# Scaling the experts' input once, and moving work between engines in both mixers of a three-layer model

## The reference, cut to what matters

```python
# layer 0: sparse attention and a state-space mixer side by side, then a gated feed-forward
h = rmsnorm(x) @ in_w                        # q, latent, index keys and queries, z, xbc, dt
y_a = attention over the 64 positions that an index score chooses (16 head-and-tile steps)
xbc = silu(causal_conv4(xbc) + conv_b)       # 12 chunks of 128 channels; then the chunked scan
x = x + concat(y_a, y_b) @ out_w
x = x + (silu(h @ w_gate) * (h @ w_up)) @ w_down
# layer 1: gated short convolution of 3 taps, then a feed-forward; final norm
x = x + (gate_b * causal_conv3(gate_c * v)) @ out_w
# layer 2: gated linear recurrence (y_a) and dilated window attention (y_b)
merged = sigmoid(ga) * (y_a @ w_branch_a) + sigmoid(gb) * (y_b @ w_branch_b)
x = x + merged @ w_out
h2 = rms_norm(x, norm2_g)
q = h2 @ peer_wq                             # 8 heads, two halves of 64
top 16 of 128 keys in each half, top 16 of the 256 sums, softmax gates
x = x + sum over experts of gelu(u[e] . h2) * gate * v[e]      # 16384 experts, all computed
```

## Time and profile before

| | us |
|---|---|
| median of 3 runs (1762.32 to 1766.17) | 1765.11 |
| the profiled execution | 1763.7 |
| its span | 1762.0 |
| TensorE busy | 1714.8 |
| ScalarE busy | 973.2 |
| VectorE busy | 1046.8 |
| GpSimd busy | 1060.3 |

### The profile page before, as it was taken

How to read it: one execution, slowest core, us unless ns; L and a number is a source line. 1 busy time by engine, 2 the same in 40 slices (tenths; PEclk the granted TensorE clock), 3 DMA queues, 4 the chain that set the end, 5 groups by cost and what they waited for, 6 DMA issues and landing times.

```text
span 1762.0 us, 32340 instructions
## 1 busy us (share of the span) xinstructions
PE 1714.8 (97%) x10886; PEld 1539.4 (87%) x10886; DVE 1046.8 (59%) x2232; ACT 973.2 (55%) x1840; POOL 1060.3 (60%) x828
## 2 busy tenths in 40 slices
PE   8989999999999999999999999999999999999999
PEld 8778788889978887989989999999999988888887
DVE  3775433336753335563532888836999866666776
ACT  5556655555455556665536545455555555555554
POOL 8435799997979998975527989897666400000000
PEclk9999999999999999999989999999999999999999
DMA  6223455554545554543424545555454555556775
GB/s 233 96 89 106 155 189 189 183 188 161 186 149 187 190 187 159 200 136 120 154 77 165 169 159 186 164 173 168 162 166 156 163 191 190 193 189 215 239 240 169
DMA packets 91852, 299.01 MB, mean 170 GB/s; under 512 B 10208, under 2 KB 22624, under 8 KB 91520
## 3 DMA queue, kind: packets, MB, share of 16 engines
q1 hardware_dynamic: 91152, 293.64, 50.4%
q0 software_dynamic: 480, 4.35, 0.7%
q10 hardware_dynamic: 144, 0.08, 0.0%
HBM read 290.69 MB, written 7.34 MB: 169 GB/s over the span
## 4 chain that ended last, share of the span: by engine, by line
PE 76%; POOL 11%; issue 6%; DVE 4%; ACT 3%; DMA 0%; POOLq 0%; DVEq 0%; SPq 0%; ACTq 0%
PE bank L683 53%; POOL w_lo L627 11%; PE bank L713 9%; PE bank L714 5%; PE bank L1298 3%; PE bank L661 1%; PE bank L1239 1%; ACT w_hi L1344 1%; PE bank L759 1%; PE bank L773 0%; DMA ring<-stream 0%; PE bank L1248 0%; DVE arena L2047 0%; PE bank L899 0%; PE bank L879 0%
## 5 line engine op out<-in xcount | busy, mean ns | idle before, releaser
L627 POOL TENSOR_TENSOR w_lo<-ring,w_hi 128x512 fp32r<-128x512 f32 x804 | 1052.7, 1319 | 334.3 <-ACT w_hi L1344 293.6
L1344 ACT ACTIVATE w_hi<-ring 128x512 fp32r<-128x512 f32 x1060 | 664.9, 632 | 641.5 <-PE bank L683 521.7
L683 PE MATMUL bank<-h_high_and_low,w_hi 128*128 128x256 f32 x3552 | 671.5, 287 | 19.7 <-POOL w_lo L627 11.7
L683 PEld LDWEIGHTS bank<-h_high_and_low,w_hi 128*128 128x128 f32 x3552 | 565.8, 193 | 24.8 <-POOL w_lo L627 12.8
L683 PE MATMUL bank<-h_high_and_low,w_lo 128*128 128x256 f32 x1776 | 505.4, 285 | 0.0
L683 PEld LDWEIGHTS bank<-h_high_and_low,w_lo 128*128 128x128 f32 x1776 | 343.3, 193 | 0.7 <-issue 0.5
L683 PE MATMUL bank<-w_hi,A_hi 128*128 128x512 f32 x728 | 287.6, 395 | 4.1 <-DVE A_lo L2221 2.8
L683 PE MATMUL bank<-w_hi,A_lo 128*128 128x512 f32 x728 | 286.5, 393 | 0.0
L683 PE MATMUL bank<-w_lo,A_hi 128*128 128x512 f32 x728 | 283.7, 390 | 0.0
L713 PE MATMUL bank<-h_high_and_low,w_hi 128*128 128x512 f32 x704 | 250.2, 398 | 0.0
L2557 DVE TENSOR_TENSOR w_lo<-ring,w_hi 128x512 fp32r<-128x512 f32 x256 | 177.1, 693 | 112.8 <-ACT w_hi L1344 111.9
(11 more groups left out here) (362 smaller groups left out, 1672.5 us busy)
## 6 DMA issues: line engine op xcount, KB each, us to landing
ring<-stream SPq DMA_DIRECT2D x530, 512.0 KB, 3.3
spill<-mask_parts SPq DMA_DIRECT2D x48, 128.0 KB, 1.7
XN<-spill SPq DMA_DIRECT2D x48, 128.0 KB, 4.7
arena<-branch_w POOLq DMA_DIRECT2D x1, 3072.0 KB, 10.3
X<-x SPq DMA_DIRECT2D x2, 512.0 KB, 4.5
arena<-kv_w SPq DMA_DIRECT2D x1, 1024.0 KB, 7.4
out<-X SPq DMA_DIRECT2D x4, 256.0 KB, 2.1
arena<-row POOLq DMA_DIRECT2D x1, 512.0 KB, 4.8
```

Of the source, the lines that this page charges most:

```text
L627: nc.gpsimd.tensor_tensor(w_lo[:, hs, :], ring[:, slot(phase, e), k * HALF:(k + 1) * HALF], w_hi[:, hs, :].bitcast(F32), ALU.subtract) \
L683: last = mm(dst, a, b, start=start and n == 0, stop=stop and n == 2, skip_group_check=True)
L1344: A(w_hi[:, half_slot(phase, e, k), :], ring[:, slot(phase, e), k * HALF:(k + 1) * HALF], ACT.Copy).then_inc(rounded, 1)
```

## The change

- First mixer: `conv` is cut in two. `scaled_input` stays on VectorE; the first tap with the bias becomes one ScalarE instruction, `first_tap`; VectorE waits for it and does the `later_taps`. `CONVS` gives the slot of each chunk. Chunks 6 and 7 go to banks 2 and 3, `cb` to bank 1. The choice of positions spreads over slots 0 to 4. On ScalarE, `conv_silu` moves from the head of slots 6 and 9 to their end, and `decay(0)` to the end of slot 10; on TensorE `cb` moves to slot 7, `cumulated(0)` to 9 and the turned inputs to 10.
- Norms: a one-column Sqrt on an unused tile `warm` stands before `high`; for the feed-forwards and the short convolution each of the two squares is followed by half of a `follow`.
- Short convolution: products and gate stay in PSUM, and ScalarE's copy of the gate is gone.
- Second mixer: the recurrence's logarithm and exponentials are halved and put behind single halves of units; outputs, sums and reciprocals come earlier; the load of `branch_w` is issued behind gate unit 12; the branch products go between the last attention steps and between the rows of `l2_out`.
- Experts: the factor is spread after four of the eight query units; `rescaled` multiplies the transposed input in PSUM, ScalarE rounds it, VectorE takes the low part, and `early` waits for it. The scaling of 128 results goes, and Gelu reads PSUM.

```diff
-X_BANKS = (6, 7, 2, 3, 6, 7, 6, 7, 6, 7, 6, 7)
+X_BANKS = (6, 7, 2, 3, 6, 7, 2, 3, 6, 7, 6, 7)
...
-    out += [("acs", 1, 1), ("BT", 1, 1), ("cb", 3, 1), ("ab0", 3, 1), ("xsT0", 1, 1), ("xsT2", 2, 1)]
+    out += [("acs", 1, 1), ("BT", 1, 1), ("cb", 1, 1), ("ab0", 3, 1), ("xsT0", 1, 1), ("xsT2", 2, 1)]
...
+        CONVS = ((), (), (0,), (1,), (2,), (3,), (4,), (5,), (6,), (7, 8), (9,), (10,))
...
+                        if p.name == "l2_gates" and e == 12:
+                            pool.wait_ge(ev("ya_ready"), 1)
+                            pool.dma_start(branch_w, br_w).then_inc(ev("branch_loaded"), 16)
                 else:
...
                         transposes("BT", [CV[:, 8 + g, 0:P] for g in range(2)])
+                    if u == 7:
                         pe.wait_ge(*before_turn("cb"))
...
+                    if u == 9:
                         cumulated(0)
-                    if u == 9:
+                    if u == 10:
                         inputs_turned(0)
...
-                        output_sums(u // 2 - 2)
+                    if u in (0, 1):
+                        outputs(u)
+                    if u in (2, 3):
+                        output_sums(u - 2)
                     if u == 1:
...
+                pe.wait_ge(ev("ya_ready"), 1)
+                pe.wait_ge(ev("branch_loaded"), 16)
+                branch_a(0)
+                attention_step("dil", NT * 4, NT * 4, logits, values)
+                branch_a(1)
+                attention_step("dil", NT * 4 + 1, NT * 4, logits, values)
+                branch_a(2)
+                pe.wait_ge(*read_out("dil_o6"))
+                pe.wait_ge(*read_out("dil_o7"))
+                transposes("ybT", [YB[:, t, cc * P:(cc + 1) * P] for cc in range(2) for t in range(NT)])
+                branch_a(3)
+                pe.wait_ge(*read_out("ybT"))
+                branch_b(0)
+                branch_b(1)
+                for k in range(4):
+                    pe.wait_ge(*before_turn(f"acc5_{k}"))
+                out_rows(0)
+                branch_b(2)
+                out_rows(1)
+                branch_b(3)
                 out_rows(2)
                 out_rows(3)
...
+                    if i == 0:
+                        spread_scale(6)
...
+                for j in range(4):
+                    pe.wait_ge(*read_out(f"hT6_{j}"))
...
+            def norm_late(n, gain, name=None):
+                A(warm[:], epst[:], ACT.Sqrt)
                 high(n, gain)
-                squares()
-            def squares():
                 for t in range(NT):
-                    A(XN[:, t, :], X[:, t, :], ACT.Square, accum_out=stat[:, t:t + 1]).then_inc(ev("ssq"), 1)
+                    square(t)
+                    if name:
+                        follow(f"{name}_head", 0, 0, (t,))
...
+                    cc = (8 + u) % 12
+                    act.wait_ge(ev("x_scaled"), u + 1)
+                    A(CV[:, cc, :], bank(f"xu{u}")[:, 0:S], ACT.Identity, bias=vcol("xbc_b", cc),
+                      scale=vcol("xbc_w", cc * 4 + 3)).then_inc(ev("first_tap"), 1)
...
                     steps = dsa_steps(u)
+                    follow("l0_feature", 4 + u, 0, (0,))
+                    for n in CONVS[u]:
+                        first_tap(n)
+                    if len(steps) == 2:
+                        attend(steps[0])
+                    follow("l0_feature", 4 + u, 0, (1,))
+                    attend(steps[-1])
                     if u == 6:
                         conv_silu(0)
                     if u == 9:
                         conv_silu(1)
                     if u == 10:
                         decay(0)
-                    follow("l0_feature", 4 + u, 0, (0,))
-                    if len(steps) == 2:
-                        attend(steps[0])
-                    follow("l0_feature", 4 + u, 0, (1,))
-                    attend(steps[-1])
                     if u == 4:
                         act.wait_ge(ev("acs_diff"), 1)
                         A(dts[:, 144:160], dts[:, 112:128], ACT.Exp)
...
                 def body(phase, e, q, turn, i, j):
-                    follow(phase, e, i)
                     if phase == f"{name}_head":
                         root(n)
+                    else:
...
-                    act.wait_ge(*unit_used(phase, e + 2, i))
-                    A(SCG[:, q, 1, :], bank(f"sc_gate{q}")[:, 0:S], ACT.Copy).then_inc(*frees(f"sc_gate{q}"))
...
                         A(qn[:], qn[:], ACT.Sqrt, bias=eps64[:]).then_inc(ev("q_rms"), 1)
+                def decay_log(j):
+                    act.wait_ge(ev("hg_f"), 1)
+                    A(HG.rearrange("p (h t) -> p h t", h=4)[:, 2 * j:2 * j + 2, :], F2[:, 2 * j:2 * j + 2, :],
+                      ACT.Ln).then_inc(ev("hg_log"), 1)
...
+                    act.wait_ge(ev("hg_sums"), 1)
+                    if j < 2:
+                        A(HT[:, half], HS[:, half], ACT.Exp).then_inc(ev("hg_exp"), 1)
+                    else:
+                        A(YA[:, half], HS[:, half], ACT.Exp, scale=-1.0).then_inc(ev("hg_exp"), 1)
...
-                    follow("l2_mix", 2 * p)
-                    if p == 6:
-                        recurrent(5)
-                    follow("l2_mix", 2 * p + 1)
+                    for e in (2 * p, 2 * p + 1):
+                        for half in range(2):
+                            follow("l2_mix", e, 0, (half,))
+                            if e == 10:
+                                decay_log(half)
+                            if p == 6:
+                                decay_exp(2 * (e % 2) + half)
                     mix_used(p)
-                    if p != 5:
-                        recurrent(p)
+                    recurrent(p)
...
                     A(F2[:, 24 + 2 * j:26 + 2 * j, :], F2[:, 24 + 2 * j:26 + 2 * j, :], ACT.Sigmoid)
...
+                for p in range(2):
+                    act.wait_ge(*read_out(f"gates{p}", 3))
+                gate_sigmoid(0)
+                attention_step("dil", NT * 4, LG1, PT1, DIL_WIDTHS)
+                gate_sigmoid(1)
+                act.wait_ge(*full("ybT"))
+                A(YBT.rearrange("p c t -> p (c t)"), bank("ybT")[:], ACT.Copy).then_inc(*frees("ybT"))
+                for j in (2, 3):
...
+                    if j < 4:
+                        act.wait_ge(ev("h_scaled"), j + 1)
+                        A(h_hi[:, 2 * j:2 * j + 2, :], bank(f"hT6_{j}")[:].rearrange("p (c t) -> p c t", t=S),
+                          ACT.Copy).then_inc(ev("scaled_high"), 1)
                     act.wait_ge(*full(f"ps{j}"))
...
                     follow(phase, at % 4, at // 4)
-                    if u >= 1:
-                        activated(u - 1)
+                    act.wait_ge(*unit_used(phase, at % 4, at // 4))
+                    A(chunk(GATED + u), bank(f"early{u % 4}")[:, 0:S], ACT.Gelu).then_inc(*frees(f"early{u % 4}"))
...
-                        act.wait_ge(*read_out(f"build{c % 3}", c // 3))
-                        A(stage[:, c % STAGED, :], stage[:, c % STAGED, :], ACT.Gelu).then_inc(ev("staged"), 1)
+                        if c >= STAGED:
+                            act.wait_ge(ev(f"spilled{c % STAGED}"), 16 * (c // STAGED))
+                        act.wait_ge(*unit_used("peer_build", e, i))
+                        A(stage[:, c % STAGED, :], bank(f"build{c % 3}")[:, 0:S],
+                          ACT.Gelu).then_inc(*frees(f"build{c % 3}"))
...
+                if n == 2:
                     chain(V.tensor_copy(RB1, bank(f"rb{n}")[:, 0:S]))
                     chain(V.tensor_tensor(RB, RB1, bank(f"rb{n}")[:, 0:S], ALU.mult))
                 else:
                     chain(V.tensor_copy(RB, bank(f"rb{n}")[:, 0:S]))
...
+            def rescaled(n, gain):
+                dve.wait_ge(ev("query_low"), 4)
+                for j in range(4):
+                    for c in range(2):
+                        v = bank(f"hT{n}_{j}")[:, c * S:(c + 1) * S]
+                        ins = V.scalar_tensor_tensor(v, v, vcol(gain, 2 * j + c), RB, ALU.mult, ALU.mult)
+                    ins.then_inc(ev("h_scaled"), 1)
+                for j in range(4):
+                    pair = slice(2 * j, 2 * j + 2)
+                    dve.wait_ge(ev("scaled_high"), j + 1)
+                    V.tensor_tensor(h_lo[:, pair, :], bank(f"hT{n}_{j}")[:].rearrange("p (c t) -> p c t", t=S),
+                                    h_hi[:, pair, :].bitcast(F32), ALU.subtract).then_inc(*frees(f"hT{n}_{j}"))
             def add_to_residual(n, phase, e, i=0):
                 for h in range(2):
...
+                def scaled_input(u):
+                    v = bank(f"xu{u}")[:, 0:S]
+                    dve.wait_ge(*unit_used("l0_feature", 4 + u))
+                    V.tensor_tensor(v, RB, v, ALU.mult).then_inc(ev("x_scaled"), 1)
+                def later_taps(u):
                     cc, name = (8 + u) % 12, f"xu{u}"
                     v, o = bank(name)[:, 0:S], CV[:, cc, :]
```

(61 more changed lines are left out.)

183 lines of the change are left out of this document (70 added, 113 removed).

## The result

The changed kernel takes 1769.73 us (median of 11 runs, 1768.87 to 1771.23); the kernel before, in the same series, 1764.25. The ratio is 1.0029, with an interval of 1.0021 to 1.0036: slower by 0.3%, where 0.4% faster was forecast. The profiled execution took 1768.9 us, its span is 1767.2, so 5.2 more than before.

A forecast was written before the change was run, and what follows sets the result against it. The prediction took TensorE to bound the kernel, busy 1714.8 of 1762.0 us. Terms 2.0 - 4.6 + 2.3 - 2.5 - 5.5 + 1.6 + 0 = -6.7 gave 1757.0 profiled, 1758.4 as median; range 1742 to 1767.

The forecast's parts named there:

- the one that gave the late stages nothing: `build` and `peer_late`: TensorE busy for 414.3 of 415 us, so sparing VectorE there is worth nothing; no term.
- Every sign that the prediction named for being right: Named waits in slots 6 and 7, loads ahead of `high`, branch products between attention steps, `w_lo` waits remaining, short-convolution wait gone.
- First mixer: Old waits and slow clock give 12.6 us, new waits, mostly for ScalarE, take 14.6: net +2.0, bounds -12.6 and +5.
- The 1.3 us that I took off: First mixer: new waits sum to 15.9 us, taken as 14.6 because a wait lets the others catch up.
- Short convolution: End of the short convolution: the wait of 2.8 us and 1.84 of slow matmuls go, -4.6, bounds -5 to -2.
- Norms: Norms: the table load before `high` falls on TensorE's path at two norms; +2.3 us in all, bounds 0 and +3.5.
- the slack of 0.6: Short convolution's norm: TensorE has about 0.6 us of slack against the 1.28 load, leaving +0.7.
- Second mixer: Recurrence and key sums: shorter waits, -2.5 us; branch products filling attention's waits at the end, -5.5.
- Experts: Hand-off before `early`: +1.6 us, bounds 0 and +4; 80 scaled results of `early` removed: 0, bounds -11.7 and +3.
- The rival that they were ScalarE's: `early`: its stalls are ScalarE's waits and vanish with the slow clock, -11.7 us, 1746.7; chance 0.17.
- the rival of 1767: `early`: GpSimd never gets its turn between two comparisons, 9 us with the clock; counted as no change, chance 0.14.
- the slower rival: First mixer: `first_tap` waits for VectorE's scaled input, each of 12 slots loses 1.2 us, +14, 1772; chance 0.08.

The follow-up runs named there:

- e2: Kernel before the change with an unused one-column tile ahead of `A_hi`, shifting it by 32 bytes: 1773.81 us, ratio 1.0055.
- e1: Changed kernel with `warm` declared behind the arena, so `A_hi` and `A_lo` lie where they lay before: 1759.25 us, ratio 0.9973 to the kernel before.
- e12: e1 with the first tap of the first mixer's convolution back on VectorE: 1755.47 us, ratio 0.9951 to the kernel before.
- e10: e1 with the old first mixer, except chunk 6 in bank 2 (later banks adapted) and the choice over five slots: 1752.73 us, ratio 0.9933.
- e6: e1 without the tile `warm` and the Sqrt on it ahead of `high`: 1758.37 us, ratio 0.9967 to the kernel before.
- e8: e1 with VectorE's 2048-element comparisons and products in the experts' choice cut into four of 512: 1752.95 us, ratio 0.9931.
- e3: Kernel before the change with an unused 16-column tile ahead of `A_hi`, putting it on a multiple of 128 bytes: 1761.94 us, ratio 0.9980.

## Why the prediction was wrong

**The step that failed is the one that gave the late stages nothing.** The prediction took the pace of a unit of rows for fixed, "that is the pace wherever nobody waits", and asked of each edit only which wait it removes or adds. The declaration of `warm` was read as nothing at all. It costs 8.3 us by the stretches: 6.8 in the last 128 units, where nobody waits, and 1.5 in the 52 rows units before. e2 shows it alone (9.6 us by the medians), e1 takes it out (10.5). With it out, the change measures 1759.25, beside a forecast of 1758.4; with it, 1769.73, over the 1767 at which the range ended. That e1 comes so near is in part luck: against their terms the first mixer is 3.9 us and the norms are 1.7 too slow there, `early` is 2.0 and `l2_mix` 1.5 too fast. Every sign that the prediction named for being right came true, and none of its signs looked at the pace of a unit.

**First mixer: the mechanism right in the main, the size wrong**, +6.3 by its stretch where +2.0 was taken. The waits for ScalarE came at the named places: at `BT` 1.5 us, behind 1.6 for VectorE that ended while ScalarE was at its table load (together 3.1, forecast 3.5), `cb` 2.3 (2.4), slot 10 2.5 (3.2); the wait at the z units was 2.8 (1.9). In the prediction's own terms, the waits were to grow by 1.6 us, from 9.4 to 11.0; TensorE's idle time in this stretch grew by 3.9, from 9.5 to 13.5. The 1.7 us of waits for VectorE's masked logits in slots 5 and 6 I had not seen; they stay in e12, so the handing over of first taps isn't their cause, and e10 has such waits too. The clock was to cost 1.7 net, and TensorE's busy time grew by 2.4: the granted clock is at half speed for 10.2 us of the stretch in both kernels, but before TensorE was idle for 3.6 of them (84.4 to 87.9 and 91.3 to 98.1 us) and now for 0.9 (95.7 to 102.5 and 106.0 to 109.4). The 1.3 us that I took off because a wait lets the others catch up are not there. e10 measures what the useful edits are worth in the old order: 3.5 us by the stretch, since waits for VectorE take back part.

**Short convolution: right**, -4.4 by its stretch and -4.7 in e1, for -4.6. From 420 to 506 us TensorE is busy throughout.

**Norms: too small.** The waits for `h_lo` are 1.7 and 1.5 (forecast 0.7 and 1.4), and the squares cut apart add 0.5 at each feed-forward: about 4 for 2.3, beyond its upper bound of 3.5. The load is nearly in full on the path (e6 gets 1.2 and 1.3 us back); the slack of 0.6 that I estimated isn't there. The Trainium skill's page "ScalarE: Activation LUTs" adds a drain to the load in "What ACT_TABLE_LOAD costs". The trace doesn't agree: the load of 405.33 takes 1.28 us, and the Sqrt begins at 406.63, 0.01 us behind it, which is also the median over the 34 loads of the changed kernel.

**Second mixer: right.** `l2_mix` -2.5, as forecast (-4.0 in the executions, e1's among them, in which it took 83.8 us). The gates and outputs gave -4.7 with the experts' norm in them, so about -6 without it, for -5.5.

**Experts: right within 2 us.** The hand-off measures +1.5 for +1.6. In `early` taking away 80 scaled results gave 2.0 and not 11.7: the wait of ScalarE is gone and the two groups of waits for `w_lo` are there, three waits a tile. The rival that they were ScalarE's (0.17) falls. So does the rival of 1767, that GpSimd never gets its turn between two comparisons: its subtraction of 1041.73 runs between two of them that stand back to back, and `early` got shorter. That the measured time lies between this rival's and the slower one's (1772) is chance: neither mechanism was there. e8 shows that they are the long comparisons: cut to 512 elements, 6.3 us come back. That is what the rule on the shared ports in the Trainium skill ("SBUF — State Buffer", "SBUF: two separate sides") says, and the trace agrees: while the two engines contend, VectorE's instructions of 2048 elements take 3.25 and 3.43 us, where one of them could take 2.29.

The forecast's range ended at 1767; the slower rival, first taps that wait for each other in every slot, was not what happened either: it would have shown in `l0_feature` as +14.

## What to carry to other kernels

Where a kernel is bound by TensorE without a wait, compare the count of matmuls in the same 100 us of both traces before looking at any wait: a tile declared in passing can move the stationary operand off its boundary, and e3 shows that the kernel before had been paying for its place too. Declare the tiles that hold stationary operands first, and check their addresses after every new declaration. Keep a table load, and every step that hands work from one engine to another, out of the stretch between TensorE's last product and what it wants next, and cut long instructions of VectorE on arrays in SBUF where GpSimd has a deadline.

## What the runs showed of the hardware

The place of the stationary operand in SBUF bears on the pace of matmuls of 128x128 by 512 columns in float32r at full clock: in `peer_late` and `peer_rest` 226.6 to 226.7 ns from start to start when its tile begins at a multiple of 128 bytes, 228.6 to 229.2 at 64 past one, 233.2 to 233.6 at 96 past one (at least two kernels each). In the rows units of the feed-forwards it is 228.5, 229.8 and 233.5 ns for the same three places. The moving operands lay in the same place throughout, and the duration that the trace gives for the loads of the stationary operand hardly changes (187 to 188 ns as a mean): only the distance from one matmul to the next shows it. Other distances, and operands in the arena, were not tried one by one. Why it is so, no run here shows.
